# Attention in steps of one query tile of two heads, with the scores of step n+2 placed in front of step n's transposes

## What is computed

```
s = q @ k.T + bias_or_mask            # 64 features per head, 96 in block two
p = softmax(concat([s, sink]))[..., :n_keys]
o = p @ v
```

## Time and profile before

| | us |
|---|---|
| median of three runs | 3055.98 (3051.24 to 3056.62) |
| the profiled execution, its own time | 3056.32 |
| its span in the trace | 3054.7 |
| PE busy | 2798.7 |
| DVE busy | 1706.7 |
| ACT busy | 1128.1 |
| POOL busy | 341.9 |

### The profile page before, as it was taken

One profiled execution on the slowest core, in us unless ns is written; L12 is line 12 of the kernel. 1 busy time (PEld: TensorE's weight loads), 2 busy tenths in 40 slices (PEclk: granted clock), 3 DMA queues, 4 the chain that ended last, 5 costly groups with the idle time before them and its releaser, 6 DMA issues.

```text
span 3054.7 us, 41358 instructions
## 1 busy us (share of the span) xinstructions
PE 2798.7 (92%) x16084; PEld 2349.2 (77%) x16084; DVE 1706.7 (56%) x2700; ACT 1128.1 (37%) x1523; POOL 341.9 (11%) x411
## 2 busy tenths in 40 slices
PE   6999989999999999999988999899569999964999
PEld 3888868757688886888874799899439999952999
DVE  4645647574672645756546655566435556544455
ACT  3222232254421224212244544444334454433443
POOL 3000131122300022000220200100001000000110
PEclk8999999899999999999998999999669999976999
DMA  6533425311352432534320255444004445410444
GB/s 240 170 139 123 160 73 206 111 32 49 105 201 86 159 123 97 207 138 156 131 104 1 73 196 182 149 177 161 14 6 177 164 174 196 160 42 0 161 164 151
DMA packets 64496, 394.20 MB, mean 129 GB/s; under 512 B 7424, under 2 KB 8928, under 8 KB 29280
## 3 DMA queue, kind: packets, MB, share of 16 engines
q1 hardware_dynamic: 41648, 310.09, 28.5%
q0 software_dynamic: 21008, 76.03, 7.3%
q10 hardware_dynamic: 1696, 6.08, 0.5%
HBM read 391.13 MB, written 1.05 MB: 128 GB/s over the span
## 4 chain that ended last, share of the span: by engine, by line
PE 81%; DVE 10%; ACT 5%; issue 2%; DMA 1%; POOL 1%; ACTq 0%; DVEq 0%; POOLq 0%
PE banks L400 21%; PE banks L402 21%; PE banks L401 21%; PE banks L1031 3%; PE banks L1050 3%; DVE wlo L365 3%; ACT whi L357 2%; PE banks L1040 2%; PE banks L425 1%; PE banks L427 1%; PE banks L426 1%; DMA shift_start<-in_w_mod 1%; PE banks L415 1%; PE banks L416 1%; PE banks L417 1%
## 5 line engine op out<-in xcount | busy, mean ns | idle before, releaser
L365 DVE TENSOR_TENSOR wlo<-raw,whi 128x2048 fp32r<-128x2048 f32 (+1 forms) x272 | 667.8, 2455 | 457.8 <-ACT whi L357 457.8
L357 ACT CAST whi<-raw 128x2048 fp32r<-128x2048 f32 (+1 forms) x272 | 548.4, 2016 | 259.5 <-PE banks L402 212.6
L400 PE MATMUL banks<-uhi,whi 128*128 128x512 f32 (+1 forms) x1648 | 601.6, 365 | 2.5 <-DVE wlo L365 2.5
L401 PE MATMUL banks<-ulo,whi 128*128 128x512 f32 (+1 forms) x1648 | 600.4, 364 | 0.0
L402 PE MATMUL banks<-uhi,wlo 128*128 128x512 f32 (+1 forms) x1648 | 600.4, 364 | 0.0
L400 PE MATMUL banks<-u2hi,whi 128*128 128x256 f32 x1312 | 371.5, 283 | 6.7 <-DVE wlo L365 4.2
L401 PE MATMUL banks<-u2lo,whi 128*128 128x256 f32 x1312 | 370.1, 282 | 0.0
L402 PE MATMUL banks<-u2hi,wlo 128*128 128x256 f32 x1312 | 369.9, 282 | 0.0
L400 PEld LDWEIGHTS banks<-uhi,whi 128*128 128x128 f32 x1648 | 309.8, 188 | 58.1 <-DVE wlo L365 3.0
L401 PEld LDWEIGHTS banks<-ulo,whi 128*128 128x128 f32 x1648 | 309.9, 188 | 54.7
L402 PEld LDWEIGHTS banks<-uhi,wlo 128*128 128x128 f32 x1648 | 309.8, 188 | 54.3
(11 more groups left out here) (363 smaller groups left out, 4274.1 us busy)
## 6 DMA issues: line engine op xcount, KB each, us to landing
raw<-in_ffn_in SPq DMA_DIRECT2D x132, 1024.0 KB, 4.8
raw<-in_ffn_out SPq DMA_DIRECT2D x48, 1408.0 KB, 6.4
mod_slot<-in_w_mod POOLq DMA_DIRECT2D x128, 512.0 KB, 3.5
raw<-in_w_merge SPq DMA_DIRECT2D x32, 1024.0 KB, 4.8
raw<-in_w_in SPq DMA_DIRECT2D x26, 1024.0 KB, 4.8
raw<-in_na_qkv SPq DMA_DIRECT2D x12, 1024.0 KB, 4.7
raw<-in_w_out SPq DMA_DIRECT2D x8, 1024.0 KB, 4.8
raw<-in_wa_qkv SPq DMA_DIRECT2D x6, 1024.0 KB, 4.7
```

What stands on the lines that cost most here:

```text
L357: act.copy(whi[u % 2][:, 0:unit_size[u]], raw[u % 2][:, 0:unit_size[u]]).then_inc(hi_done, 1)
L365: dve.tensor_tensor(wlo[u % 2][:, 0:n], raw[u % 2][:, 0:n], whi[u % 2][:, 0:n].bitcast(F32), ALU.subtract).then_inc(lo_done, 1)
L400: pe.matmul(out, w_hi, x_hi[:, k, 0:T], start=(n == 0), stop=False)
L401: pe.matmul(out, w_hi, x_lo[:, k, 0:T], start=False, stop=False)
```

## The change

A unit of work is now a step: the same 128 queries of both heads of a pair, called sides 0 and 1. There are half as many steps as there were tiles: 32 in layer 0 (in fours: two with 512 keys, two with 256), 16 in layer 1, 4 in each stage of block two.

- PE's order in iteration n is scores(n+2) of both sides, transposes(n) of both sides, values(n-1) of both sides. Scores wait once, for the exponentials of step n-2, and then both sides follow without a wait. Transposes wait for the copies of step n-1, for the division of side 0, and in the middle for that of side 1. Values wait once, for both copies of the step.
- Scores of side 0 and 1 have banks 0 and 1, or 4 and 5, in turn; the transposes have bank 2 for side 0 and 3 for side 1, and no longer alternate between steps.
- DVE does M of both sides of step n, then N of both sides of step n-1. ACT does both exponentials of step n, then both copies of step n-1.
- Since two sides of two steps are alive, `probs_t` of odd steps and the bias of odd pairs lie in `mod_slot`. ACT waits for the end of the modulation products, which use it, ahead of two attention stages.
- POOL loads both biases of a pair, two pairs ahead, and adds the mask to both in succession.
- The last `y_hi` and `y_lo` of a pair come two and three iterations behind its last step (before: three and four).

The number of products, transposes, exponentials, maxima, divisions and copies, and their sizes, stay the same.

```diff
+    def probs(n, side):
+        return (scaled, sums)[n % 2][:, side]
+
+    def probs_t(n, side, w):
+        if w > S:
+            return (full_u, mod_slot[:, 1].rearrange("p (a b) -> p a b", a=2))[n % 2][:, side]
+        return full_u[:, n % 2, side * S:(side + 1) * S]
...
+    na_bias = (squares, mod_slot[:, 0].rearrange("p (a b) -> p a b", a=2))
...
+    def score_bank(n, side):
+        return 4 * (n % 2) + side
+
+    def attention_pe(pe, tag, steps):
         def scores(n):
-            t = tiles[n]
-            if n >= 4:
-                pe.wait_ge(*ACT_.at(tag, "exp", n - 4))
-            pe.matmul(banks[:, score_bank(n), 0:t["n"]], t["q"], t["k"], start=True, stop=True)\
-                .then_inc(*PE_.up((tag, "scores", n)))
+            if n >= 2:
+                pe.wait_ge(*ACT_.at(tag, "exp", n - 2))
+            for side, t in enumerate(steps[n]["tiles"]):
+                pe.matmul(banks[:, score_bank(n, side), 0:steps[n]["n"]], t["q"], t["k"], start=True, stop=True)\
+                    .then_inc(*PE_.up((tag, "scores", n)))
 
         def transposes(n):
-            t = tiles[n]
-            pe.wait_ge(*DVE_.at(tag, "probs", n))
-            if n >= 2:
-                pe.wait_ge(*ACT_.at(tag, "probs_t", n - 2))
...
+            w = steps[n]["n"]
+            if n >= 1:
+                pe.wait_ge(*ACT_.at(tag, "probs_t", n - 1))
+            for side in range(2):
+                pe.wait_ge(*DVE_.at(tag, "probs", n, side))
+                for j in range(w // P):
+                    mm = pe.transpose(banks[:, 2 + side, j * P:(j + 1) * P], probs(n, side)[:, j * P:(j + 1) * P],
+                                      ident)
+                mm.then_inc(*PE_.up((tag, "transposed", n, side)))
...
-        for n in range(N + 2):
+        for n in range(N + 1):
             if n + 2 < N:
                 scores(n + 2)
-            if 1 <= n <= N:
-                transposes(n - 1)
-            if n >= 2:
-                values(n - 2)
...
             if n < N:
...
+                transposes(n)
+            if n >= 1:
+                values(n - 1)
...
+        load_pair(0)
+        load_pair(1)
+        mask = c("na_mask").rearrange("p (o c) -> p o c", o=1).to_broadcast([P, T2 // GRID_W, GRID_W])
+        for ck in range(KC):
+            for side in range(2):
+                pool.wait_ge(bias_loaded[ck % 2][side], 16 * (ck // 2 + 1))
+                bias = na_bias[ck % 2][:, side, :].rearrange("p (r c) -> p r c", c=GRID_W)
+                pool.tensor_tensor(bias, bias, mask, ALU.add).then_inc(*POOL_.up(("bias", 2 * ck + side)))
+            if 1 <= ck < KC - 1:
+                pool.wait_ge(*DVE_.at("L0", "added", 4 * (ck - 1) + 1, 1))
+                load_pair(ck + 1)
```

More of the change, by code:

```diff
@@ L322, in build @@
     mla_loaded = sem("mla_weights_loaded")
-    bias_loaded = [sem("na_bias_loaded_0"), sem("na_bias_loaded_1")]
+    bias_loaded = [[sem(f"na_bias_loaded_{i}_{side}") for side in range(2)] for i in range(2)]
     stored = sem("output_stored")
@@ new lines, in attention_act @@
+    def attention_act(act, tag, steps, y_hi):
+        N = len(steps)
+        for n in range(N + 2):
+            if n < N:
+                w = steps[n]["n"]
+                for side, t in enumerate(steps[n]["tiles"]):
+                    i = 2 * (n % 2) + side
+                    act.wait_ge(*DVE_.at(tag, "max", n, side))
+                    if n >= 2:
+                        act.wait_ge(*PE_.at(tag, "transposed", n - 2, side))
+                    act.activation(probs(n, side)[:, 0:w], banks[:, score_bank(n, side), 0:w], ACT.Exp,
+                                   bias=small[:, i:i + 1], accum_out=small[:, 4 + i:5 + i])\
+                        .then_inc(*ACT_.up((tag, "exp", n) if side else (tag, "exp of first", n)))
+                    if t["sink"] is not None:
+                        act.activation(small[:, 8 + i:9 + i], t["sink"], ACT.Exp, bias=small[:, i:i + 1])\
+                            .then_inc(*ACT_.up((tag, "sink", n, side)))
@@ L1089, in attention_act @@
+            if n >= 2 and steps[n - 2]["last"]:
+                t = steps[n - 2]
+                act.wait_ge(*PE_.at(tag, "values", n - 2))
                 w = t["width"]
@@ L1139, in attention_dve @@
+            if n >= 3 and steps[n - 3]["last"]:
+                t = steps[n - 3]
                 dve.wait_ge(*ACT_.at(tag, "out", t["group"]))
@@ L1983, in _ @@
         qkv_act(act, "L1", S)
[L1984 removed]
+        act.wait_ge(mod_done, 2 * (MOD_CHUNKS - KC))
+        attention_act(act, "L1", wa_steps(), uhi)
         out_act(act, "L1.wo", 5, S)
```

238 lines of the change are left out of this document (108 added, 130 removed).

## The result

The changed kernel takes 2976.02 us (median of four runs, 2975.19 to 2976.82). The kernel before took 3053.61 (four runs, 3050.74 to 3056.62): the ratio is 0.9746, with a 95% interval of 0.9729 to 0.9763. The forecast was 2998, its range 2981 to 3032.

A forecast was written before the change was run, and what follows sets the result against it. PE was taken as the bound before the change, DVE after it in the large stages. Savings of 37 us (layer 0), 19 (layer 1) and 2 (block two), 58 off 3056.3, gave 2998 us, range 2981 to 3032.

The forecast's parts named there:

- The overlap: Scores and values on PE: both heads of a step run at once and cost what one head costs now.
- (c): PE: MATMULs start strictly in program order, only neighbours overlap; a pair takes 14.4 us, in all 3032 us; chance 0.09.
- (d): PE: no overlap at all, only fewer waits; a pair takes 15.5 us, in all 3048 us; chance 0.04.
- By that rule the values get nothing: Values on PE: under the skill's program-order rule they gain no overlap, and the time is that of (c).
- Values of sixteen: Values on PE, steps of 512 keys: sixteen MATMULs of two heads cost 1.01 us; called less sure than scores.
- the sign that the prediction named as speaking against it: Layer 1 at full clock: PE working without pause would show the overlap fell short and the forecast wrong.
- DVE as the bound: Both large stages: the bound moves from PE to DVE, 12.2 us per pair in layer 0, 3.77 per layer 1 step.
- POOL's additions: Layer 0: mask additions slow DVE divisions beside them, taken as 2.1 us per pair, between nothing and 2.7.
- The half clock: Start of both large stages: 1.2 GHz kept until 602.1 and 1632.9, with 19.2 us per pair, 6.0 per step.
- (e): Clock rises some 15 us earlier in layer 0, 6 in layer 1, and POOL's additions cost little: 2983 us; chance 0.10.
- The number of steps: Both large stages: all 8 pairs and 16 steps counted after the first transposes, plus about 2 us at the end.
- The covered waits: Attention stages: new waits for copies, scores' exponentials, POOL's loads and ACT's extra waits put at nothing.

The follow-up runs named there:

- The serial run: Changed kernel with side 1 waiting for side 0's last product in both scores and values, so the heads can't overlap: 3054.64 us against 3055.28, ratio 0.9991.

## Why the forecast was right in sign and too small

**The overlap (right).** That two heads run at the same time on PE, from the rows of `sb_pe`, was the main step. Scores measured 1.06 against 1.05 forecast, values of eight 0.59 against 0.58. The serial run shows that nearly all of the gain hangs on it. Rivals (c) and (d), with only neighbours overlapping or nothing, are out. The Trainium skill (TensorE: Matmul & The Clock Gate, "Part 3: Packing small matmuls") lets MATMULs start and end in program order only. The trace disagrees for these shapes: in blocks of eight per side strict order would give (c)'s 1.87 us and 1.51 were measured, in blocks of four 1.01 and 0.59. The prediction's "By that rule the values get nothing" went further than that section, which reports a gain from packing by columns too.

**Values of sixteen (too low).** Forecast 1.01, measured 1.51. The doubt stood in the prediction, and I took the better end. PE's step of layer 1 is 3.59, not 3.24, and a pair 10.8, not 10.4. So the sign that the prediction named as speaking against it, PE without a pause in layer 1, did show: in six steps the profile has PE busy for 22.22 of 22.23 us and no wait. DVE has none either. The two are that close: every second group of eight transposes took 1.24 us (1595.49 to 1596.73) in place of 1.02, which fits a wait in its middle for the division of side 1, begun at 1595.60.

**DVE as the bound (right number, wrong reason).** Forecast 12.2 per pair and 3.77 per step, measured 11.88 and 3.71. But POOL's additions were put at 2.1 us per pair, and they cost DVE 0.43 and the pair nothing. In their place stand waits: in two of four iterations PE is the slower one (1.05 + 0.59 + 1.51 = 3.15, or 0.64 + 1.02 + 1.51 = 3.17, against DVE's 2.2 and 2.7), in the other two DVE is (3.0 and 2.9 against 2.24). The two errors nearly cancelled, which was luck.

**The half clock (the step that failed most).** "Until 602.1 I keep the half clock as it was." It ended at 582.1. The forecast charged 1.14 pairs at 19.2 in place of 11.88, 8.3 us, and 1.5 steps at 6.0 in place of 3.71 in layer 1, 3.4 us. The half clock that was left cost about 0.3 us in layer 0 and 1.2 in layer 1, by the first distances between groups of transposes (2.64 us in place of 2.31; 3.91 + 4.74 in place of 2 x 3.71). Rival (e) had the right direction, with a chance of 0.10. What ended it sooner isn't shown. In layer 0 the stretch at 1.2 GHz was 3.4 us in the changed kernel, 10 with both parts serial and with the scores serial, 7 with the values serial or in turn, and 24 in the kernel before; it was 14 with PE one step later and 3.4 in both runs with alternating steps. It was 7 with the short mask addition too, where PE's work is that of the changed kernel, so a few us of it are scatter. Neither the overlap alone nor PE's being busy explains the rest: with both parts serial nothing overlaps and the clock was back after 10 us, while the kernel before was busy 22.45 of 22.46 us at 1.2 GHz. These are single traces, and the same kernel differs from run to run: over 13 runs the kernel before had a mean granted clock between 0.938 and 0.946, while the four of the changed kernel had 0.945 or 0.946. So how much of the 20 us belongs to the change, and what in the change does it, remains open.

**The number of steps (failed).** The forecast let all 8 pairs and all 16 steps pass after the first transposes. But by then DVE has already done the maxima of steps 0 and 1, and from the first transposes to the last there are only N - 1 steps. With the measured periods its own formula gives 8 x 11.88 + 2 = 97.0 us from 580.24, and 92.3 were measured; in layer 1 16 x 3.71 + 2 = 61.4 from 1572.39, against 59.2. Together 4.7 + 2.2 = 6.9 us. The missing step is 2.97 us of it in layer 0 and 3.71 in layer 1. The rest is at the ends: no scores stand before the last two groups of transposes, which come 2.1 us sooner for it in layer 0 and 1.1 in layer 1; against that, the end took 3.5 us after the last transposes in layer 1, not 2, and the half clock that was left counts too.

**Sum of the miss.** Layer 0: 114.7 forecast, 99.5 measured; 8.3 for the half clock, 4.7 for the count, 2.2 for the period. Layer 1: 72.9 and 66.2; 3.4, 2.2 and 0.9 (14.5 steps at 3.77 for 3.71). Block two saved 2.4 and 1.6 where 1 and 1 were forecast. The first transposes came at 580.24 (forecast 580.3) and 7.0 us into layer 1 (7.0), so the start itself was right. The range was too narrow below: its best case (e) let the clock rise 15 us earlier in layer 0, where 20 were measured, and made POOL's additions cheap, which gave 2983, and the count stood in no case at all.

**The covered waits (right).** In the middle of both stages PE waits for no copy of line 1094, for no POOL operation and no load; its only waits are the six for DVE above, and none that the profile shows in the six steps of layer 1. The run with PE one step later shows what the copies cost when the cover is gone.

## What to carry to other kernels

When two engines hand a chain of steps back and forth in strict order, compare their work iteration by iteration and add up the larger ones; the larger of the two sums is only a lower bound, and matching heavy with light iterations, or moving one operation to another iteration, can be worth as much as making it faster (0.56 us per pair here for moving 0.69 us of work, 0.34 for a short division). Two heads on different halves of TensorE's rows or columns can cost what one costs (1.06 us for 1.05, 1.03 for 1.01), if no wait stands between them and, for long groups, if their products are issued in turn. And count a pipeline's steps from what is already done when the clock of your sum starts.

## What was not expected of the hardware

- Sixteen value MATMULs of two heads took 1.51 us in blocks of eight and 1.03 in turn, eight of them 0.59 even in blocks of four.
- A MATMUL that waits for the product just ahead of it on PE costs some 0.1 us more than the work (2.23 against 2 x 1.05).
- POOL's division of 128x512 took 1.56 us, where DVE's division takes 0.40 from start to start.
- A DVE division beside POOL's addition took 0.90 us with 256 columns and 0.91 to 1.14 with only 2, in place of 0.35 and 0.23: what is lost didn't depend on the division's length.
- The stretch at 1.2 GHz at the start of layer 0 lasted from 3.4 to 24 us among kernels that do the same work there, each in one trace.
